# Time steps projected ahead of z, and their sums, columns and the scan's first transposes made beside the projection of z

## The chip, the cores and the metric

The kernel runs on one core of one Trainium2 chip. The metric is the device time of one execution in microseconds; the kernel before was run three times.

## The reference, cut to what matters

One step of an encoder layer on 512 new tokens of a prompt and 64 of a running stream: a mixer, attention over memory tokens, and a mixture of 16 experts. The change is in the mixer's state-space (Mamba-2) branch:

```python
h = rmsnorm(x, norm_mix)
z, xbc_raw, dt_raw, q, k, v, gl_ssm, gl_sb = split_cols(h @ w_in)
xbc = silu(causal_conv(xbc_raw))                    # 1536 channels: x, B, C
dt = softplus(dt_raw + dt_bias)                     # 16 heads: the time steps
a = -exp(a_log)
cum = cumsum(dt * a)                                # in blocks of positions
y, h_last = ssd_chunked(xh, dt, a, bm, cm, ssm_h0)  # the scan
y = y + d_skip[:, None] * xh
y_ssm = rmsnorm(y * silu(z), ssm_norm) @ w_ssm_br   # z: 1024 channels
```

So the scan needs dt and the convolved x, B, C; z is needed only where the scan's output is multiplied by it.

## The kernel before, in words

All 576 tokens (T = 512 + 64) are kept transposed, channels in the partitions, in 8 blocks of 128 channels (KD). The kernel writes its engines' programs out by hand: each engine runs its list in order, and semaphores are the only links between them.

**Weights.** `w_in` is cut into tiles of 8 x 128 x 256 words (or 128 columns), numbered in the order of use: K, V, Q, X (six tiles, 1536 columns of x, B, C), Z (four tiles, 1024 columns), DT (one tile, 128 columns, of which 16 are the time steps), then two tiles for each of the 8 merge steps (W_M on). SP loads tile n into one of four ring slots once tile n - 4 has been used for the last time (`load`, L1280; the table `retire`, L468). Each product is made in three passes of a high and a low part: `split_high` (L417, cast at L422) writes the high part on ScalarE, into one of two slots, once tile n - 2 has been used; `split_low` (L424, at L428) subtracts it in place on VectorE.

**Projections.** `tproj` (L1988, matmuls at L1985) makes 128 output channels of all tokens: 2 halves of 288 tokens x 8 blocks x 3 passes = 48 matmuls, the halves in two neighbouring PSUM banks. X takes 12 such steps, Z 8, DT one; they alternate between banks 0, 1 and banks 2, 3. For X, ScalarE copies out (L1483 to L1485), VectorE makes the convolution (L1728 to L1732), and ScalarE applies Silu (L1491). For Z, ScalarE applies Silu on the way out of PSUM (L1495) and signals `zt_ready`. After the last z step TensorE makes the columns of the D skip (L2160) and transposes the rows kept for the convolution (L2165), then the time steps' projection, and then transposes the initial state (L2175) once `dve_dt` 1 says that the time steps have been read.

**Row chain.** The time steps are 16 rows. VectorE adds the bias (L1750); ScalarE applies Abs, Exp and Ln (L1501 to L1505); VectorE adds the parts (L1757), multiplies by a (L1761), makes the sums by a scan instruction (L1763) and a diagonal of the last ones (L1766, `dve_dt` 7), and splits the sums in three bf16 parts (L1768 to L1776, `dve_dt` 12). TensorE turns sums and steps into columns (L2180, L2181) and spreads the last ones over all partitions (L2182); VectorE copies them out and copies the state (L1783), and ScalarE applies two exponentials (L1509, L1511).

**The scan** has 10 steps: 5 blocks of up to 128 tokens x 2 groups of 8 heads. In TensorE's order `ssd_first` of step v + 1 stands ahead of `ssd_second` of step v. `ssd_first` (L2197 to L2205) transposes x and B, makes the product of B and C, and spreads the sums. ScalarE makes decays from them (L1518, eight of L1520, L1524), GpSimd one product (L1386), VectorE the operands (`xdt`, L1797 to L1801) and the masked decays (L1811). `ssd_second` (L2219 to L2231) accumulates the output in bank 3 and the state in bank 6; VectorE multiplies the output into z (L1820) and updates the state (L1823, L1827). Banks: 7 and 0 for `ssd_first`, 1, 2 and 4, 5 in turn for the spread sums. VectorE does the low half of tile W_M + 1 in step 0. After the scan the final states are transposed (L2245) and the merge begins.

## Time and profile before

| | us |
|---|---|
| median of 3 runs | 1280.15 |
| lowest and highest run | 1276.65, 1280.24 |
| the profiled execution's own time | 1275.22 |
| its span | 1273.4 |
| TensorE busy (matmul) | 1159.3 (91%) |
| VectorE busy | 721.1 (57%) |
| ScalarE busy | 569.6 (45%) |
| GpSimd busy | 119.8 (9%) |
| mean granted clock of TensorE | 0.954 |

The profile is of one execution; its times count from the span's start. An engine's busy share says how long it had something running, not whether that was what the next work waited for. Overlapping matmuls are counted once, and their ends are modelled. In a timeline each row merges instructions of one line; the bracket gives the engine's idle time ahead of it and what ended that.

### The profile page before, as it was taken

What the parts mean: (1) busy time and instruction counts of PE and PEld (TensorE: products, weight loads), DVE (VectorE), ACT (ScalarE), POOL (GpSimd) and SP (SyncE); (2) the same over time, 40 slices, a digit from 0 to 9 for tenths busy, and PEclk for the clock granted to TensorE, in tenths of its full rate; (3) what the DMA queues carried; (4) which work ended last, traced back from release to release, by engine and by line L of the source; (5) the groups of instructions that cost most, each with busy time, mean ns of one, the idle gap of its engine ahead of it and who ended that gap; (6) DMA issues with size and microseconds to landing.
All of it is one profiled execution on the core that took longest, in us unless ns stands there. A gap on an engine that the chain in (4) does not pass through costs nothing.

```text
span 1273.4 us, 18213 instructions
## 1 busy us (share of the span) xinstructions
PE 1159.3 (91%) x7804; PEld 1041.8 (82%) x7813; DVE 721.1 (57%) x832; ACT 569.6 (45%) x704; POOL 119.8 (9%) x131
## 2 busy tenths in 40 slices
PE   5998997999969999999899899789769999899995
PEld 4997687999957899999899899469747777778873
DVE  5312764664168843342434713633478998888884
ACT  4423562332247642222315523421156687677763
POOL 1000431000034200000000000000010110000031
PEclk9998887999979999999999999999869999999998
DMA  8432000231310133332526612000389999999996
GB/s 277 137 105 66 1 1 17 67 96 55 83 35 2 34 91 83 81 93 68 174 68 221 210 38 84 12 17 34 130 317 339 422 399 385 360 395 392 366 286 155
DMA packets 95004, 197.24 MB, mean 155 GB/s; under 512 B 4184, under 2 KB 71928, under 8 KB 82632
## 3 DMA queue, kind: packets, MB, share of 16 engines
q1 hardware_dynamic: 87328, 169.88, 38.3%
q0 software_dynamic: 5408, 18.76, 5.0%
q10 hardware_dynamic: 2184, 7.39, 1.4%
q8 instruction: 63, 1.03, 0.3%
q14 instruction: 21, 0.17, 0.0%
HBM read 178.41 MB, written 17.60 MB: 154 GB/s over the span
## 4 chain that ended last, share of the span: by engine, by line
PE 69%; DVE 20%; ACT 7%; issue 3%; DMA 1%; POOL 0%; SPq 0%; ACTq 0%; DVEq 0%; POOLq 0%
PE ps L1985 44%; DVE buf_r L847 9%; PE ps L909 6%; PE ps L919 2%; ACT buf_r L840 2%; PE ps L2352 1%; PE ps L2103 1%; DVE buf_r L1028 1%; PE ps L2104 1%; DMA buf<-in_w_in 1%; PE ps L2074 1%; PE ps L539 1%; DVE buf L577 1%; PE ps L893 1%; ACT buf_r L422 1%
## 5 line engine op out<-in xcount | busy, mean ns | idle before, releaser
L1985 PE MATMUL ps<-buf_r,buf_r 128*128 128x288 f32 (+1 forms) x4560 | 595.5, 292 | 12.8 <-DVE buf_r L438 9.7
L1985 PEld LDWEIGHTS ps<-buf_r,buf_r 128*128 128x128 f32 x4560 | 589.1, 190 | 14.7 <-issue 5.9
L428 DVE TENSOR_TENSOR buf_r<-buf,buf_r 128x2048 fp32r<-128x2048 f32 (+2 forms) x53 | 116.6, 2200 | 174.8 <-ACT buf_r L422 174.8
L847 DVE TENSOR_TENSOR buf_r<-buf,buf_r 128x2048 fp32r<-128x2048 f32 x96 | 213.9, 2283 | 0.0
L909 PE MATMUL ps<-buf_r,buf_r 128*128 128x512 f32 x768 | 187.7, 400 | 6.9 <-DVE buf_r L1028 6.9
L840 ACT CAST buf_r<-buf 128x2048 fp32r<-128x2048 f32 x96 | 178.8, 1908 | 12.8 <-DMA buf<-in_w_gate_e 11.3
L909 PEld LDWEIGHTS ps<-buf_r,buf_r 128*128 128x128 f32 x768 | 144.0, 191 | 38.3 <-DVE buf_r L1028 7.7
L422 ACT CAST buf_r<-buf 128x2048 fp32r<-128x2048 f32 (+2 forms) x53 | 96.6, 1823 | 117.2 <-PE ps L1985 65.9
L919 PE MATMUL ps<-buf_r,buf_r 128*128 128x512 f32 x384 | 92.4, 395 | 2.5 <-DVE buf_r L1052 1.4
L919 PEld LDWEIGHTS ps<-buf_r,buf_r 128*128 128x128 f32 x384 | 71.8, 188 | 20.4 <-DVE buf_r L847 2.4
L434 ACT CAST buf_r<-ps 128x1024 fp32r<-128x1024 f32 (+1 forms) x32 | 25.7, 802 | 75.4 <-PE ps L893 66.7
L519 ACT ACTIVATE buf<-buf 128x1024 f32<-128x1024 f32 (+1 forms) x22 | 23.2, 1056 | 66.0 <-DVE buf L1966 48.1
L1074 POOL DMA_INDIRECT buf<-hn_rows,buf x16 | 23.3, 1453 | 270.2 <-DVE buf L583 135.2
L2103 PE MATMUL ps<-buf_r,buf_r 128*128 128x256 f32 (+1 forms) x78 | 30.0, 394 | 7.1 <-DVE buf_r L1678 7.1
L434 ACT CAST buf_r<-buf 128x576 fp32r<-128x576 f32 (+4 forms) x28 | 24.3, 869 | 23.6 <-DVE buf L1860 11.6
L438 DVE TENSOR_TENSOR buf_r<-buf,buf_r 128x576 fp32r<-128x576 f32 (+4 forms) x28 | 27.6, 999 | 10.2 <-ACT buf_r L434 10.2
L539 PE MATMUL ps<-buf,buf 128*128 128x128 f32 (+1 forms) x136 | 19.6, 296 | 12.2 <-DVE buf L529 9.5
L1386 POOL TENSOR_TENSOR buf<-buf,buf 128x1024 f32<-128x1024 f32 x10 | 27.9, 2785 | 29.5 <-ACT buf L1518 29.5
L1732 DVE SCALAR_TENSOR_TENSOR buf<-buf,buf,buf 128x579 f32<-128x579 f32 x36 | 29.6, 822 | 1.3
L1483 ACT COPY buf<-ps 128x288 f32<-128x288 f32 x12 | 4.8, 400 | 55.2 <-PE ps L1985 55.2
L2074 PE MATMUL ps<-buf,buf 64*128 64x512 f32 (+3 forms) x64 | 24.8, 540 | 4.6 <-DVE buf L1668 3.2
L1028 DVE TENSOR_TENSOR buf_r<-ps,buf_r 128x1024 fp32r<-128x1024 f32 x16 | 19.5, 1221 | 15.6 <-ACT buf_r L434 15.6
(313 smaller groups left out, 1208.6 us busy)
## 6 DMA issues: line engine op xcount, KB each, us to landing
buf<-in_w_gate_e SPq DMA_DIRECT2D x32, 1024.0 KB, 8.4
buf<-in_w_up_e SPq DMA_DIRECT2D x32, 1024.0 KB, 7.9
buf<-in_w_down_e SPq DMA_DIRECT2D x32, 1024.0 KB, 7.5
buf<-in_w_in SPq DMA_DIRECT2D x16, 1024.0 KB, 5.7
buf<-in_w_in SPq DMA_DIRECT2D x17, 512.0 KB, 4.7
buf<-in_w_mem_kv SPq DMA_DIRECT2D x8, 1024.0 KB, 5.7
y_rows<-buf ACTq DMA_DIRECT2D x14, 512.0 KB, 8.6
buf<-in_x_prompt SPq DMA_DIRECT2D x8, 512.0 KB, 5.3
```

Source lines behind the costliest of these rows:

```text
L422: nc.scalar.copy(w_hi(n), tile_view(RAW[n % NRAW], n)).then_inc(wh_ready, 1)
L428: nc.vector.tensor_tensor(r32(raw), raw, w_hi(n), ALU.subtract).then_inc(wl_ready, 1)
L434: nc.scalar.copy(r32(hi), src).then_inc(ah_ready, 1)
L539: last = nc.tensor.transpose(norm_banks(i, b0)[:, c, 0:n], src[:, c * P:(c + 1) * P], IDENT[:n, :n])
L840: nc.scalar.copy(e_hi(t), e_raw(t)).then_inc(wh_ready, 1)
L847: nc.vector.tensor_tensor(e_lo(t), e_raw(t), e_hi(t), ALU.subtract).then_inc(wl_ready, 1)
L909: last = nc.tensor.matmul(bank(b), r32(a[:, k, :]), w[:, i, :], start=(k == 0 and j == 0), stop=(k == KD - 1 and j == 2))
L919: last = nc.tensor.matmul(bank(5 + c), r32(a[:, k, :]), w[:, i, 512 * c:512 * (c + 1)], start=(k == 0 and j == 0), stop=(k == 3 and j == 2))
L1028: nc.vector.tensor_tensor(r32(GT[e % 2]), bank(0, 2).rearrange("p (c n) -> p c n", c=KD), r32(GTH[e % 2]), ALU.subtract).then_inc(al_ready, 1)
L1985: last = nc.tensor.matmul(out, a, b, start=(k == 0 and j == 0), stop=(k == len(parts) - 1 and j == 2))
L2074: last = nc.tensor.matmul(ps[:, o:o + n], KTA[r, hp, kc * P:(kc + 1) * P], QT[r, hp, kc * P:LP], start=True, stop=True)
L2103: nc.tensor.matmul(out, m, high[:, oj:oj + nj], start=(j == kc), stop=False)
```

## The change

The time steps' weight tile is numbered ahead of z's four, so it is loaded, split and projected between X and Z. z's eight steps use banks 3, 4 and 5, 6 in place of 0 to 3 (the last one 3 and 6), which leaves out banks 0, 1, 2 and 7; `tproj` takes a second bank. TensorE's order becomes: time steps, z0, D columns, tail transposes, state transposes, z1, z2, columns and spread, z3 to z6, `ssd_first(0)`, z7, then the scan as before, whose `ssd_second(0)` also waits for z7's Silu. ScalarE does the three row functions ahead of z0's Silu, the two exponentials behind z4's, z7's behind its part of scan step 0, and the cast of tile W_M + 1 behind its part of step 2. Silu is made in two instructions, one per bank. VectorE has the row chain ahead of and between the low halves of z's tiles, and the low half of W_M + 1 in step 4. The diff:

```diff
--- before.py
+++ after.py
@@ -385,8 +385,8 @@
         W_V = add_tiles(w_in, C_V, 512)
         W_Q = add_tiles(w_in, C_Q, 512)
         W_X = add_tiles(w_in, C_X, CONV_C * P)
+        W_DT = add_tiles(w_in, C_DT, P, P)
         W_Z = add_tiles(w_in, C_Z, D)
-        W_DT = add_tiles(w_in, C_DT, P, P)
         W_M = len(tiles)
         for c in range(0, D, P):
             tiles.append(([(0, cols(w_in, C_GS + c, P)), (8, cols(w_in, C_GB + c, P))], P))
@@ -1410,6 +1410,8 @@
             act_high(HTH[:, :, t0:t0 + n], HT[:, :, t0:t0 + n])
 
 
+        Z_BANK = [(3, 4), (5, 6)] * 3 + [(3, 4), (3, 6)]
+
         def cum_banks(v):
             return bank(1 if v % 2 == 0 else 4, 2).rearrange("p (h t) -> p h t", h=8)
 
@@ -1490,12 +1492,6 @@
                     act.wait_ge(conv_done, j + 1)
                     nc.scalar.activation(XC[:, j, 0:LP], CV[j % 2][:, 0:512], ACT.Silu)
                     nc.scalar.activation(XC[:, j, LP:T], CV[j % 2][:, 515:579], ACT.Silu).then_inc(xc_ready, 1)
-            for i in range(KD):
-                act.wait_ge(zt_psum, i + 1)
-                nc.scalar.activation(halves(ZS[:, i, :]), pair(2 * (i % 2)), ACT.Silu).then_inc(zt_ready, 1)
-                if i % 2:
-                    split_high(act, W_Z + 2 + i // 2)
-
             exp_and_ln()
             act.wait_ge(dve_dt, 1)
             nc.scalar.activation(AD[0:NH, :], UD[0:NH, :], ACT.Abs).then_inc(act_dt, 1)
@@ -1504,11 +1500,23 @@
             act.wait_ge(act_dt, 2)
             nc.scalar.activation(AD[0:NH, :], AD[0:NH, :], ACT.Ln, bias=1.0).then_inc(act_dt, 1)
             nc.scalar.activation(HCOL[0:NH, 3:4], HCOL[0:NH, 1:2], ACT.Exp).then_inc(act_dt, 1)
-            split_high(act, W_M + 1)
-            act.wait_ge(pre_dve, 4)
-            nc.scalar.activation(TE, TE, ACT.Exp).then_inc(pre_act, 1)
-            act.wait_ge(pre_psum, 2)
-            nc.scalar.activation(CD, bank(7)[:, 160:240].rearrange("p (c h) -> p c h", c=NC_), ACT.Exp).then_inc(pre_act, 1)
+            split_high(act, W_Z + 1)
+
+            def z_out(i):
+                act.wait_ge(zt_psum, i + 1)
+                for h in range(2):
+                    last = nc.scalar.activation(ZS[:, i, T // 2 * h:T // 2 * (h + 1)], bank(Z_BANK[i][h])[:, 0:T // 2], ACT.Silu)
+                last.then_inc(zt_ready, 1)
+
+            for i in range(KD - 1):
+                z_out(i)
+                if i in (1, 3, 5):
+                    split_high(act, W_Z + 2 + i // 2)
+                if i == 4:
+                    act.wait_ge(pre_dve, 4)
+                    nc.scalar.activation(TE, TE, ACT.Exp).then_inc(pre_act, 1)
+                    act.wait_ge(pre_psum, 2)
+                    nc.scalar.activation(CD, bank(7)[:, 160:240].rearrange("p (c h) -> p c h", c=NC_), ACT.Exp).then_inc(pre_act, 1)
             for v in range(10):
                 c, g = divmod(v, 2)
                 act.wait_ge(cumb_psum, v + 1)
@@ -1522,6 +1530,10 @@
                 last.then_inc(seg_done, 1)
                 act.wait_ge(seg_done, v + 1)
                 nc.scalar.activation(SEG[v % 2], SEG[v % 2], ACT.Exp, scale=-1.0).then_inc(e_ready, 1)
+                if v == 0:
+                    z_out(KD - 1)
+                if v == 2:
+                    split_high(act, W_M + 1)
             act.wait_ge(intra_psum, 10)
             act_high(YSBTH, YSBT)
             act.wait_ge(so_psum, 2)
@@ -1735,9 +1747,8 @@
                     o.then_inc(conv_step if j < 3 else conv_done, 1)
                 if i % 2:
                     split_low(dve, W_X + 2 + i // 2)
-            for n in range(W_Z + 2, W_M + 1):
-                split_low(dve, n)
-
+            dve.wait_ge(dt_psum, 1)
+            nc.vector.tensor_scalar(halves(UD[0:NH, :]), pair(0, NH), HCOL[0:NH, 0:1], None, ALU.add).then_inc(dve_dt, 1)
             dve.wait_ge(vec_ready, 3)
             for r in (0, 32, 64):
                 nc.vector.tensor_copy(SEL3[r:r + NH, :], IDENT[r:r + NH, r:r + NH])
@@ -1745,14 +1756,13 @@
             nc.vector.tensor_copy(DP, bank(7)[:, 240:248]).then_inc(vec_ready, 1)
             for s in range(2):
                 dve.wait_ge(dp_psum, 3)
-                nc.vector.tensor_copy(TAILR[0:36, s, :], bank(6)[0:36, P * s:P * (s + 1)]).then_inc(tail_rows, 1)
-            dve.wait_ge(dt_psum, 1)
-            nc.vector.tensor_scalar(halves(UD[0:NH, :]), pair(0, NH), HCOL[0:NH, 0:1], None, ALU.add).then_inc(dve_dt, 1)
+                nc.vector.tensor_copy(TAILR[0:36, s, :], bank(2)[0:36, P * s:P * (s + 1)]).then_inc(tail_rows, 1)
 
             nc.vector.memset(DTT[0:NH, T:TS], 0.0)
             nc.vector.memset(RST[0:NH, :], 1.0).then_inc(dve_dt, 1)
             dve.wait_ge(dve_dt, 2)
             nc.vector.memset(RST[0:NH, :].rearrange("p (c t) -> p c t", t=P)[:, :, 0:1], 0.0).then_inc(dve_dt, 1)
+            split_low(dve, W_Z + 1)
             dve.wait_ge(act_dt, 3)
             nc.vector.scalar_tensor_tensor(out=DTT[0:NH, 0:T], in0=UD[0:NH, :], scalar=0.0, in1=AD[0:NH, :],
                                            op0=ALU.max, op1=ALU.add).then_inc(dve_dt, 1)
@@ -1774,18 +1784,21 @@
             nc.vector.tensor_tensor(RST[64:64 + NH, :], DTA[32:32 + NH, :], CUM3[32:32 + NH, :], ALU.subtract).then_inc(dve_dt, 1)
             dve.wait_ge(dve_dt, 11)
             nc.vector.tensor_copy(CUM3[64:64 + NH, :], RST[64:64 + NH, :]).then_inc(dve_dt, 1)
+            split_low(dve, W_Z + 2)
             dve.wait_ge(pre_psum, 2)
             p7 = lambda a: bank(7)[:, a:a + 80].rearrange("p (c h) -> p c h", c=NC_)
             nc.vector.tensor_copy(CR, p7(0)).then_inc(pre_dve, 1)
             nc.vector.tensor_copy(DR, p7(80)).then_inc(pre_dve, 1)
             dve.wait_ge(pre_psum, 1)
             dve.wait_ge(pads, 2)
-            nc.vector.tensor_copy(HS[:, 1], bank(1, 2).rearrange("p (g n) -> p g n", g=2)).then_inc(pre_dve, 1)
+            nc.vector.tensor_copy(HS[:, 1], bank(0, 2).rearrange("p (g n) -> p g n", g=2)).then_inc(pre_dve, 1)
             dve.wait_ge(pre_dve, 3)
             nc.vector.tensor_tensor(TE, p7(160), CR, ALU.subtract).then_inc(pre_dve, 1)
+            split_low(dve, W_Z + 3)
             dve.wait_ge(pre_act, 2)
             nc.vector.tensor_tensor(WRW, DR, TE, ALU.mult).then_inc(pre_dve, 1)
             dve.wait_ge(pre_dve, 5)
+            split_low(dve, W_M)
 
             def xdt(v):
 
@@ -1812,10 +1825,12 @@
                                         ALU.mult).then_inc(m_ready, 1)
                 if v < 9:
                     xdt(v + 1)
-                if v == 0:
+                if v == 4:
                     split_low(dve, W_M + 1)
                 dve.wait_ge(intra_psum, v + 1)
                 n = CH[c][1]
+                if v == 1:
+                    dve.wait_ge(zt_ready, KD)
                 zv = ZS[:, 4 * g:4 * g + 4, c * P:c * P + n]
                 nc.vector.tensor_tensor(zv, zv, bank(3).rearrange("p (j t) -> p j t", j=4)[:, :, 0:n],
                                         ALU.mult).then_inc(yz_done, 1)
@@ -1985,11 +2000,11 @@
                     last = nc.tensor.matmul(out, a, b, start=(k == 0 and j == 0), stop=(k == len(parts) - 1 and j == 2))
             return last
 
-        def tproj(b, n, c, high, low, nk=KD, k0=0):
+        def tproj(b, n, c, high, low, nk=KD, k0=0, b2=None):
 
             for h in range(2):
                 t = slice(h * (T // 2), (h + 1) * (T // 2))
-                last = passes(bank(b + h)[:, 0:T // 2], [((w_hi(n)[:, k0 + k, c:c + P], w_lo(n)[:, k0 + k, c:c + P]),
+                last = passes(bank(b2 if h and b2 else b + h)[:, 0:T // 2], [((w_hi(n)[:, k0 + k, c:c + P], w_lo(n)[:, k0 + k, c:c + P]),
                                      (r32(high[:, k, t]), r32(low[:, k, t]))) for k in range(nk)])
             return last
 
@@ -2145,15 +2160,22 @@
                 if i >= 2:
                     pe.wait_ge(xr_ready, i - 1)
                 tproj(2 * (i % 2), W_X + i // 2, (i % 2) * P, HTH, HT).then_inc(xb_psum, 1)
-            for i in range(KD):
+            pe.wait_ge(wl_ready, W_DT + 1)
+            pe.wait_ge(xr_ready, CONV_C - 1)
+            tproj(0, W_DT, 0, HTH, HT).then_inc(dt_psum, 1)
+
+            def z_rows(i):
                 if i % 2 == 0:
                     pe.wait_ge(wl_ready, W_Z + i // 2 + 1)
-                if i < 2:
-                    pe.wait_ge(xr_ready, CONV_C - 1 + i)
-                else:
-                    pe.wait_ge(zt_ready, i - 1)
-                tproj(2 * (i % 2), W_Z + i // 2, (i % 2) * P, HTH, HT).then_inc(zt_psum, 1)
-
+                if i == 0:
+                    pe.wait_ge(xr_ready, CONV_C)
+                if i == 1:
+                    pe.wait_ge(ysb_ready, 5)
+                if i >= 2:
+                    pe.wait_ge(zt_ready, i - 1 if i < KD - 1 else i)
+                tproj(Z_BANK[i][0], W_Z + i // 2, (i % 2) * P, HTH, HT, b2=Z_BANK[i][1]).then_inc(zt_psum, 1)
+
+            z_rows(0)
             pe.wait_ge(vec_ready, 4)
             pe.wait_ge(ysb_ready, 5)
             for j in range(8):
@@ -2162,18 +2184,15 @@
             last.then_inc(dp_psum, 1)
             pe.wait_ge(conv_done, CONV_C)
             for s in range(2):
-                nc.tensor.transpose(bank(6)[0:36, P * s:P * (s + 1)], TAIL[:, s].rearrange("p j c -> p (j c)"),
+                nc.tensor.transpose(bank(2)[0:36, P * s:P * (s + 1)], TAIL[:, s].rearrange("p j c -> p (j c)"),
                                     IDENT).then_inc(dp_psum, 1)
-            pe.wait_ge(wl_ready, W_DT + 1)
-            pe.wait_ge(zt_ready, 7)
-            tproj(0, W_DT, 0, HTH, HT).then_inc(dt_psum, 1)
-
             pe.wait_ge(state_loaded, 16)
             pe.wait_ge(dve_dt, 1)
-            pe.wait_ge(zt_ready, 8)
             for b in range(8):
-                last = nc.tensor.transpose(bank(1, 2)[:, b * P:(b + 1) * P], H0R[:, b, :], IDENT)
+                last = nc.tensor.transpose(bank(0, 2)[:, b * P:(b + 1) * P], H0R[:, b, :], IDENT)
             last.then_inc(pre_psum, 1)
+            z_rows(1)
+            z_rows(2)
             pe.wait_ge(dve_dt, 7)
             pe.wait_ge(vec_ready, 5)
             for c in range(NC_):
@@ -2181,6 +2200,8 @@
                 nc.tensor.transpose(bank(7)[:, 80 + 16 * c:96 + 16 * c], DTT[0:NH, c * P:(c + 1) * P], IDENT[0:NH, 0:NH])
             nc.tensor.matmul(bank(7)[:, 160:240], ONES[0:NH, :], DIAG[0:NH].rearrange("p c h -> p (c h)"),
                              start=True, stop=True).then_inc(pre_psum, 1)
+            for i in range(3, KD - 1):
+                z_rows(i)
             pe.wait_ge(pre_dve, 4)
             pe.wait_ge(pre_act, 2)
             pe.wait_ge(xc_ready, CONV_C)
@@ -2216,6 +2237,7 @@
                 else:
                     pe.wait_ge(dd_ready, 2)
                     pe.wait_ge(pads, 3)
+                    pe.wait_ge(zt_ready, KD)
                 nc.tensor.matmul(bank(3), ZERO[:, 0:P], ZERO, start=True, stop=False)
                 for j in range(4):
                     nc.tensor.matmul(bank(3)[:, j * P:(j + 1) * P], DD[g][:, j, :], XC[:, 4 * g + j, tk], start=False, stop=False)
@@ -2233,6 +2255,7 @@
                 last.then_inc(intra_psum, 1)
 
             ssd_first(0)
+            z_rows(KD - 1)
             for v in range(10):
                 if v + 1 < 10:
                     ssd_first(v + 1)
```

## Rows read from the trace of the kernel before

**Rows 1.** The page, part 4: the chain that ended last, shares of the span.

```profile
PE 69%; DVE 20%; ACT 7%; issue 3%; DMA 1%; POOL 0%; SPq 0%; ACTq 0%; DVEq 0%; POOLq 0%
```

**Rows 2.** Timeline of TensorE before the scan: start, duration, operation, idle time before it.

```profile
346.04 1.94 PE L2160 MATMUL ps<-buf,buf 16*128 16x1 f32 x16
...
348.06 6.60 PE L1985 MATMUL ps<-buf_r,buf_r 128*128 128x288 f32 x48
355.61 1.06 PE L2175 MATMUL ps<-buf,buf 128*128 128x128 f32 x8 [0.94 <-issue]
360.91 0.28 PE L2180 MATMUL ps<-buf,buf 16*128 16x16 f32 x1 [4.24 <-DVE buf L1766]
...
367.20 1.09 PE L2197 MATMUL ps<-buf,buf 128*128 128x128 f32 x4 [4.51 <-ACT buf L1511]
...
370.77 1.11 PE L2197 MATMUL ps<-buf,buf 128*128 128x128 f32 x4 [0.99 <-DVE buf L1801]
```

**Rows 3.** Timeline of TensorE in the scan.

```profile
379.97 1.05 PE L2221 MATMUL ps<-buf,buf 128*128 128x128 f32 x8 [0.33 <-DVE buf L1820]
...
384.27 1.09 PE L2231 MATMUL ps<-buf,buf 128*64 128x128 f32 x16 [1.16 <-DVE buf L1811]
385.86 0.66 PE L2197 MATMUL ps<-buf,buf 128*128 128x128 f32 x4 [0.50 <-DVE buf L1801]
...
387.36 1.05 PE L2221 MATMUL ps<-buf,buf 128*128 128x128 f32 x8
...
391.44 0.66 PE L2197 MATMUL ps<-buf,buf 128*128 128x128 f32 x4
...
428.81 1.09 PE L2231 MATMUL ps<-buf,buf 128*64 128x128 f32 x16
```

**Rows 4.** Stretches: length, busy times (instructions) of each engine, granted clock, DMA.

```profile
348.00:354.70 6.70, 6.66 (x50) 6.42 (x50) 3.25 (x7) 1.87 (x2) 1.07 (x2) 1.00 0.57 152
...
360.90:367.20 6.30, 1.78 (x13) 1.60 (x13) 4.88 (x10) 0.40 (x2) 3.09 (x4) 0.50 0.00 0
...
378.00:386.00 8.00, 6.00 (x64) 4.49 (x62) 7.90 (x10) 4.21 (x11) 2.36 (x1) 1.00 0.00 0
```

**Rows 5.** Timeline of ScalarE around the projection of z.

```profile
295.16 0.40 ACT L1483 COPY buf<-ps 128x288 f32<-128x288 f32 x1 [4.94 <-PE ps L1985]
...
301.53 0.65 ACT L1495 ACTIVATE buf<-ps 128x576 f32<-128x576 f32 x1 [1.47 <-PE ps L1985]
...
346.69 1.89 ACT L422 CAST buf_r<-buf 128x2048 fp32r<-128x2048 f32 x1
...
369.81 1.02 ACT L1518 ACTIVATE buf<-ps 128x1024 f32<-128x1024 f32 x1 [2.72 <-PE ps L2205]
...
372.94 1.06 ACT L1524 ACTIVATE buf<-buf 128x1024 f32<-128x1024 f32 x1
```

**Rows 6.** Timeline of VectorE, same stretch and the scan's start.

```profile
299.17 2.29 DVE L428 TENSOR_TENSOR buf_r<-buf,buf_r 128x2048 fp32r<-128x2048 f32 x1
...
354.70 0.81 DVE L1750 TENSOR_SCALAR buf<-ps,buf 16x576 f32<-16x576 f32 x1 [2.80 <-PE ps L1985]
...
360.62 0.23 DVE L1766 TENSOR_TENSOR buf<-buf,buf 16x80 f32<-16x80 f32 x1
...
376.76 2.33 DVE L428 TENSOR_TENSOR buf_r<-buf,buf_r 128x1536 fp32r<-128x1536 f32 x1
...
381.00 3.21 DVE L1811 TENSOR_TENSOR buf<-buf,buf 128x1024 f32<-128x1024 f32 x1
...
387.71 1.22 DVE L1811 TENSOR_TENSOR buf<-buf,buf 128x1024 f32<-128x1024 f32 x1
```

**Rows 7.** Timeline of GpSimd at the scan's second step.

```profile
380.78 2.36 POOL L1386 TENSOR_TENSOR buf<-buf,buf 128x1024 f32<-128x1024 f32 x1 [3.30 <-ACT buf L1518]
```

**Rows 8.** Timeline of ScalarE behind the scan.

```profile
446.02 1.28 ACT L1545 ACT_TABLE_LOAD   x1
447.31 0.65 ACT L1545 ACTIVATE buf<-ps 128x576 f32<-128x576 f32 x1
```

## The prediction

> **What bounds the kernel now.** I read the page's chain first: TensorE carries 69% of what ended last [rows 1], so time is to be had where TensorE stands still and something else is last. TensorE's timeline ahead of the scan shows three such places: 0.94 us before the state's transposes, 4.24 us before the columns, 4.51 us before the scan, and 0.99 us more before the scan's second step [rows 2]. In sum 10.68 us. The releasers named are VectorE's row chain (L1766), the exponentials on ScalarE (L1511) and VectorE's operands (L1801): the reader is to see a serial chain over 16 rows that starts only when the time steps are out of PSUM. The scan's timeline comes next, for the pace of its undisturbed steps and for three smaller stops of 0.33, 1.16 and 0.50 us [rows 3]. Last the granted clock by stretches: 1.00 until 354.7, 0.50 in 360.9 to 367.2 with TensorE busy 1.78 of 6.3 us, 1.00 again from 378 [rows 4]. So the stops also make TensorE slow behind them: the same four transposes take 1.09 us at 367.2 and 0.66 us at 385.9 [rows 2, 3].
>
> **The stretch that I sum.** It begins where the last x/B/C projection is done, which the copy at 295.16 shows [rows 5], and ends with the scan's last matmuls at 428.81 + 1.09 = 429.90 [rows 3]: 134.7 us. Before it nothing is changed but the order of two tile loads. Behind it the same waits follow the scan's end.
>
> **TensorE's work after the change, in its new order.** One projection of 128 columns takes 301.53 - 295.16 = 6.37 us [rows 5]. Nine of them (time steps and z0 to z7) are 57.3 us. The D-skip columns and tail transposes are 348.06 - 346.04 = 2.0 us, the state's transposes 1.1 [rows 2], the columns 1.8 (busy time in that stretch) [rows 4]. In the scan a "first" takes 387.36 - 385.86 = 1.50 us and a "second" 391.44 - 387.36 = 4.08 us at full clock [rows 3]. First(0) to first(3) and second(0) and (1) are 4 x 1.50 + 2 x 4.08 = 14.2 us; from second(2) at 387.36 to 429.90 I take the 42.5 us as they are, with what waits they hold. Sum 118.9 us. The durations of the small groups are taken whole, though behind another matmul their tails overlap; that may give 0.5 us more.
>
> **Does a wait take the place of the old ones?** I lay the new order on the clock of the old trace.
> - Time steps 295.2 to 301.5. z0 needs the low half of z's first tile. Tile 13 is still the one split at 299.17 + 2.29 = 301.46 [rows 6], and is now needed at once, not one tile later: TensorE's start hangs on it with 0.05 us to spare. I put 0.1 us there, between 0 and 0.5.
> - z0 ends at 307.9, small groups and state at 311.1. The state's transposes wait for the time steps to leave banks 0 and 1: 0.81 us on VectorE [rows 6], so by 302.4, long before.
> - z1 to 317.5. z2 needs tile 14. ScalarE does the three 16-row functions first (576 columns each, as Silu's 0.65 us [rows 5], so some 2.1 us, to 304.5), then the cast, 1.89 us. VectorE stands at the D columns until TensorE has passed z0 (309.9). Of its 3.25 busy us in 348.0 to 354.7 the copies there were 1.0 beside a low half of 2.29 [rows 4, 6]; the memsets I put at 1 more. Ready at 309.9 + 2.0 + 2.3 = 314.2, 3.3 us early.
> - z2 to 323.9. The columns need dve_dt 7. The row chain was 354.70 to 360.62 + 0.23 = 360.85, 6.15 us in all [rows 6]; without the first row (0.81) and ScalarE's 2.1 it has 3.2 left behind the low half, so 317.4: 6.5 us early. The 4.24 us stop goes. The three-part sums behind it are asked for at 351 only.
> - z3 from 325.7, z4 at 332.0. Its tile waits for z1 to retire (317.5), then Silu, cast and low half, 0.7 + 1.9 + 2.3: 322.4, 9.6 us early. z6 at 344.8 has its tile from z3's end at 332.0 + 4.9 = 336.9, 7.9 us early. The wait of z by its banks is for the step two before, and the copy-out is 0.65 us [rows 5].
> - The exponentials of TE and CD come behind z4's Silu, at about 341, ten us before the scan. The 4.51 us stop goes. z6 ends at 351.1.
> - First(0) to 352.6, then z7 to 359.0. Beside z7 ScalarE does its whole first scan step, 374.00 - 369.81 = 4.2 us [rows 5], and VectorE its operands: the 0.99 us goes. z7's Silu must be out before second(0), which TensorE reaches at 360.5: it ends about 0.75 us after z7, at 359.8. ScalarE's second step then ends by about 365.2 with VectorE 1.2 us behind it; second(1) asks for it 3.1 us after 366, at 369.
>
> **Table loads.** Silu and Exp now alternate, by my reading of the new order six more switches than before, each 1.28 us, with the next function 0.01 us after it [rows 8]. They stand ahead of the semaphore wait in ScalarE's idle time, or behind a step that has 6.37 us of cover. In the scan two of them count, one on either side of z7's Silu; with 1.28 us each they meet the times above (ScalarE free at 357.5, table at 358.8). Uncovered, the two would be 2.6 us. I take 0.
>
> The Trainium skill ("ScalarE: Activation LUTs", What ACT_TABLE_LOAD costs) gives each switch about 1.28 us and a drain of about 1.38 us more, which speaks against this change. Rows 8 show the first and not the second. By the page, z7's Silu would end 0.4 us after second(0) is reached, and the sum below would be 0.4 us smaller. I go by the rows.
>
> **The stops inside the scan.** Before, VectorE did the low half of the second branch tile (L428, 2.33 us, GpSimd's share in it included) in step 0. With it VectorE came late, met GpSimd's product at 380.78 (2.36 us) and took 3.21 us for one at 381.00 that takes 1.22 at 387.71 [rows 6, 7]; TensorE stopped 0.33 + 1.16 + 0.50 = 1.99 us [rows 3]. The change moves this low half to step 4. It stands at the same place of its step there, behind the next step's operands, so I expect the same meeting and the same 1.99 us there: moved, not saved. Bounds 0 and 4 us. On ScalarE the cast of that tile moves behind step 2 (1.5 us, against 5.58 - 4.2 = 1.4 us free per step): nothing waits for that.
>
> **SP's queue.** Each load waits for the tile four before it. With the time steps' tile in front, the loads of the later tiles are released by z1, z3, z5 and z7 at the latest; none is needed within 10 us. Cost 0.
>
> **Sum.** 118.9 + 0.1 + 2.0 = 121.0 us against 134.7 us: 13.7 us less. Of it 10.7 are the idle times of rows 2, and 3.0 are the low clock, which has no stop left to follow. The profiled execution took 1275.22 us (span 1273.4), so it would take 1261.5. The median of the three runs is 4.9 us above that execution; 1280.15 - 13.7 = 1266.4, and I predict 1266 us.
>
> **Rivals.**
> - *Half of it comes back in the scan.* The first steps run late on ScalarE and VectorE because z7, its Silu, two tables and the delayed steps crowd there, and the low half in step 4 costs the upper bound. 2.6 + 2 + 2 us are 6.6 us back: 1273 us. For it: VectorE's waits in the scan are short, and 0.2 us of bad phase cost 2.0 us there [rows 6, 7]. Against: 6.4 us of z7 lie over step 0. Chance 0.16.
> - *The change does not do what it says*: the chain still ends after TensorE is through, because VectorE, in one queue, is held by the D columns, pads or a tile. It would have to be 6.5 us later than I find at the columns and over 9 us at the exponentials. Then about 10 us remain of the stops: 1278 us. Chance 0.06.
> - *Slower: the clock falls in the middle of z.* The mechanism: the 16-row matmuls, transposes and waits now stand between z0 and z1 and between z2 and z3, and the clock falls there as it fell at 355 to 361. At the low level a projection takes 6.37 x (1.09 / 0.66) = 10.5 us, 4.1 us more. From four such steps on it is slower than before; with five, 1266 + 21 = 1287 us. Against it: through 348.0 to 354.7, right behind the same small matmuls, the clock stayed at 1.00 [rows 4]. Chance 0.03.
>
> **How the numbers follow.** The forecast has 0.75. Its own range is the sum's bounds: 0.5 us of overlap and 2.0 us of step 4 gained, 2 to 3 us lost there and at z0, and the 3 us by which runs of this kernel differ: 1260.5 to 1271. Reached out to the first rival the range is 1260.5 to 1274. Runs of this kernel tell differences from about 0.3%, 3.8 us: faster holds the forecast, the first rival and a little of the second (0.91), same most of the second (0.06), slower the third (0.03).
>
> **What would show it.** In the new profile: no idle time of TensorE over 0.3 us between 295 and the scan; the time steps' projection at 295.2 with its row function at 301.5; clock 1.00 in every stretch from 295 to 430; z7's projection between first(0) and first(1); the last scan matmuls ending at about 416; a VectorE product of some 3 us and stops of about 2 us at step 4; everything behind the scan moved up by the same 13.7 us. The prediction is wrong if TensorE stands at z2, z4 or z6, if ScalarE's first steps in the scan are what second(0) or second(1) waits for, or if the stages behind the scan give time back.

## The result and the profile after

The changed kernel's median was 1263.39 us (4 runs, 1255.01 to 1266.45) against 1278.40 us (4 runs): ratio 0.9899, interval 0.986 to 0.9937. A second set of 6 runs beside 11 of the kernel before gave 0.9906 (0.9872 to 0.9941). The profiled execution took 1261.06 us, its span 1259.3. Forecast were 1266 us, and 13.7 us less in the stretch from the end of the x/B/C projection to the end of the scan.

The whole is noisy, its parts are not. First the kernel before, then the changed one, by stages between the same events: the tail of the attention (unchanged), the stretch, the merge's start, and a part of the expert stage. Columns as in [rows 4].

```profile
191.00:223.00 32.00, 24.86 (x210) 22.84 (x209) 14.20 (x18) 7.52 (x6) 4.72 (x4) 0.80 0.06 17
...
295.16:429.90 134.74, 120.91 (x1042) 107.53 (x1050) 73.40 (x113) 62.09 (x128) 32.34 (x16) 0.94 0.15 40
429.90:457.40 27.50, 25.47 (x191) 24.53 (x189) 20.31 (x26) 21.86 (x26) 1.88 (x2) 1.00 0.29 77
...
959.67:1100.00 140.33, 134.19 (x659) 107.07 (x658) 127.82 (x122) 99.38 (x71) 13.28 (x10) 1.00 0.99 387
```

```profile
191.00:219.20 28.20, 21.06 (x210) 18.96 (x210) 14.45 (x18) 7.52 (x6) 4.73 (x4) 0.96 0.06 19
...
291.34:411.60 120.26, 117.18 (x1042) 104.21 (x1051) 73.61 (x113) 71.26 (x142) 32.98 (x16) 1.00 0.18 49
411.60:439.10 27.50, 25.47 (x190) 24.53 (x189) 20.32 (x26) 21.85 (x26) 1.88 (x2) 1.00 0.29 77
...
942.52:1085.00 142.48, 135.90 (x660) 108.35 (x659) 129.66 (x123) 99.40 (x72) 13.30 (x10) 0.99 0.98 382
```

The stretch went from 134.74 to 120.26 us, 14.5 less, with TensorE busy 117.2 of 120.3 us and the clock at 1.00, not 0.94. The attention's tail was 3.8 us shorter, with the clock at 0.96 and not 0.80, before any changed instruction; the merge's start was equal; the later stages were 4.2 us longer, of which 2.2 in the piece shown. These two nearly cancel in this pair of profiles, which is luck. The last experiment shows that the first is chance, and leaves open whether some 2 us of the second are.

TensorE in the changed kernel. `tproj`'s matmuls are at L2000 now, the D columns at L2182, the state's transposes at L2192, the sums' columns at L2199 to L2201, `ssd_first` at L2218 to L2226, `ssd_second` at L2243 to L2253.

```profile
304.25 1.94 PE L2182 MATMUL ps<-buf,buf 16*128 16x1 f32 x16
...
306.36 1.04 PE L2192 MATMUL ps<-buf,buf 128*128 128x128 f32 x8
307.15 12.96 PE L2000 MATMUL ps<-buf_r,buf_r 128*128 128x288 f32 x96
320.04 0.23 PE L2199 MATMUL ps<-buf,buf 16*128 16x16 f32 x1
...
320.69 0.42 PE L2201 MATMUL ps<-buf,buf 16*128 16x80 f32 x2
321.04 25.76 PE L2000 MATMUL ps<-buf_r,buf_r 128*128 128x288 f32 x192
346.63 0.60 PE L2218 MATMUL ps<-buf,buf 128*128 128x128 f32 x4
...
347.82 6.62 PE L2000 MATMUL ps<-buf_r,buf_r 128*128 128x288 f32 x48
354.29 0.60 PE L2218 MATMUL ps<-buf,buf 128*128 128x128 f32 x4
...
355.72 1.05 PE L2243 MATMUL ps<-buf,buf 128*128 128x128 f32 x8
...
384.61 1.05 PE L2243 MATMUL ps<-buf,buf 128*128 128x128 f32 x8 [1.04 <-DVE buf L1835]
...
388.29 1.09 PE L2253 MATMUL ps<-buf,buf 128*64 128x128 f32 x16 [0.55 <-DVE buf L1824]
389.88 0.66 PE L2218 MATMUL ps<-buf,buf 128*128 128x128 f32 x4 [0.50 <-DVE buf L1814]
...
410.51 1.09 PE L2253 MATMUL ps<-buf,buf 128*64 128x128 f32 x16
```

The rows up to 384 have no bracket, so TensorE has no idle time to speak of between 304 and 384, where [rows 2] had 0.94, 4.24, 4.51 and 0.99 us. Two projections lie between the state's transposes and the columns, four (25.76 us) up to the scan, z7 (6.62 us) between the first two `ssd_first`, and the four transposes take 0.60 us, not 1.09. The three stops of [rows 3], 0.33 and 1.16 us in `ssd_second(1)` and 0.50 us ahead of `ssd_first(3)`, are now 1.04 and 0.55 us in `ssd_second(5)` and 0.50 us ahead of `ssd_first(7)`, one step behind the low half, which VectorE now does in its step 4. The scan ends at 410.51 + 1.09 = 411.60.

ScalarE beside it: row functions, cast, and Silu with its table changes.

```profile
298.56 0.69 ACT L1497 ACTIVATE buf<-buf 16x576 f32<-16x576 f32 x1 [1.01 <-DVE buf L1751]
...
300.68 1.89 ACT L422 CAST buf_r<-buf 128x2048 fp32r<-128x2048 f32 x1
302.59 1.28 ACT L1508 ACT_TABLE_LOAD   x1
304.36 0.71 ACT L1508 ACTIVATE buf<-ps 128x288 f32<-128x288 f32 x2 [0.48 <-PE ps L2000]
...
334.81 1.28 ACT L1517 ACT_TABLE_LOAD   x1
336.11 0.27 ACT L1517 ACTIVATE buf<-buf 128x80 f32<-128x80 f32 x1
...
353.06 1.28 ACT L1508 ACT_TABLE_LOAD   x1
354.49 0.71 ACT L1508 ACTIVATE buf<-ps 128x288 f32<-128x288 f32 x2
355.21 1.28 ACT L1526 ACT_TABLE_LOAD   x1
356.51 1.02 ACT L1526 ACTIVATE buf<-ps 128x1024 f32<-128x1024 f32 x1
```

The table load at 302.59 stands ahead of its wait for z0. The two in the scan (353.06, 355.21) lie around z7's Silu, which is out at 355.20, half a microsecond ahead of the first "second" at 355.72.

### The profile page after: what moved, and what is told of

It is laid out like the page before. It is cut to its first block, busy times and chain, and to the rows that moved or that the text cites. A ratio compares the mean times of both kernels' runs of the same rounds, so it can differ in the third digit from the quotient of the medians.

```text
span 1259.3 us, 18228 instructions
## 1 busy us (share of the span) xinstructions
PE 1157.4 (92%) x7804; PEld 1038.5 (82%) x7813; DVE 720.4 (57%) x832; ACT 578.0 (46%) x718; POOL 120.2 (10%) x131
## 4 chain that ended last, share of the span: by engine, by line
PE 69%; DVE 19%; ACT 6%; issue 3%; DMA 1%; POOL 0%; SPq 0%; ACTq 0%; DVEq 0%; POOLq 0%
PE ps L2000 45%; DVE buf_r L847 9%; PE ps L909 6%; PE ps L919 2%; ACT buf_r L840 2%; PE ps L2375 1%; PE ps L2118 1%; DVE buf_r L1028 1%; DMA buf<-in_w_in 1%; PE ps L2089 1%; PE ps L2119 1%; PE ps L539 1%; DVE buf L577 1%; PE ps L893 1%; ACT buf_r L422 1%
## 5 line engine op out<-in xcount | busy, mean ns | idle before, releaser
L2000 PE MATMUL ps<-buf_r,buf_r 128*128 128x288 f32 (+1 forms) x4560 | 598.1, 293 | 12.8 <-DVE buf_r L438 9.7
L2000 PEld LDWEIGHTS ps<-buf_r,buf_r 128*128 128x128 f32 x4560 | 591.1, 191 | 15.0 <-issue 5.9
L909 PE MATMUL ps<-buf_r,buf_r 128*128 128x512 f32 x768 | 189.0, 402 | 7.1 <-DVE buf_r L1028 7.1
L422 ACT CAST buf_r<-buf 128x2048 fp32r<-128x2048 f32 (+2 forms) x53 | 96.7, 1824 | 117.2 <-PE ps L2000 65.9
L919 PE MATMUL ps<-buf_r,buf_r 128*128 128x512 f32 x384 | 94.0, 400 | 2.6 <-DVE buf_r L1052 1.4
L1462 ACT ACTIVATE buf<-buf 128x1280 f32<-128x1280 f32 x10 | 12.7, 1270 | 35.1 <-POOL buf L1352 18.7
```

What stands on the lines that cost most here:

```text
L422: nc.scalar.copy(w_hi(n), tile_view(RAW[n % NRAW], n)).then_inc(wh_ready, 1)
L909: last = nc.tensor.matmul(bank(b), r32(a[:, k, :]), w[:, i, :], start=(k == 0 and j == 0), stop=(k == KD - 1 and j == 2))
L919: last = nc.tensor.matmul(bank(5 + c), r32(a[:, k, :]), w[:, i, 512 * c:512 * (c + 1)], start=(k == 0 and j == 0), stop=(k == 3 and j == 2))
L2000: last = nc.tensor.matmul(out, a, b, start=(k == 0 and j == 0), stop=(k == len(parts) - 1 and j == 2))
```

## The experiments

Each was read by its stretch, from the last 288-column copy of the x/B/C projection to the scan's last matmul. This has next to no scatter: three profiles of the kernel before gave 134.74 or 134.75 us each, two of the changed kernel 120.25 and 120.28.

**Stops without the low clock.** Dummy matmuls in both long stops of the kernel before:

```diff
             last.then_inc(pre_psum, 1)
+            for _ in range(28):
+                nc.tensor.matmul(bank(5)[:, 0:T // 2], r32(HTH[:, 0, 0:P]), r32(HTH[:, 0, 0:T // 2]), start=True, stop=True)
             pe.wait_ge(dve_dt, 7)
 ...
                              start=True, stop=True).then_inc(pre_psum, 1)
+            for _ in range(30):
+                nc.tensor.matmul(bank(5)[:, 0:T // 2], r32(HTH[:, 0, 0:P]), r32(HTH[:, 0, 0:T // 2]), start=True, stop=True)
             pe.wait_ge(pre_dve, 4)
```

> The kernel before, with 28 matmuls of 128x288 (133 ns each) into an unused bank behind the state's transposes and 30 behind the columns; nothing reads them. They fill TensorE's two long stops (4.24 and 4.51 us) without shortening what is waited for. Theory: of the 14.5 us that the changed kernel saved between the x/B/C projection and the scan's end, about 3 are the low clock behind the stops. Then here the clock stays at 1.00 over the whole stretch, the chain of VectorE and ScalarE takes the same time, and the stretch (134.7 us) falls by 2.5 to 3.5 us, to about 131.7. Rival: the clock behind the stops costs nothing by itself, because the first scan steps wait for VectorE and ScalarE anyway: stretch 134.7, scan's second step at the same distance from the row chain.

Stretch 133.68 us: 1.1 less, not 3. Time 0.9975 of the kernel before (0.995 to 0.9999). Its TensorE, VectorE and GpSimd:

```profile
362.20:368.40 6.20, 5.21 (x42) 4.90 (x42) 4.80 (x9) 0.40 (x2) 2.99 (x4) 1.00 0.00 0
...
371.30:376.00 4.70, 4.64 (x43) 3.61 (x46) 1.86 (x4) 4.67 (x14) 3.06 (x2) 1.00 0.00 0
...
368.49 0.63 PE L2201 MATMUL ps<-buf,buf 128*128 128x128 f32 x4 [1.07 <-DVE buf L1785]
...
371.30 0.66 PE L2201 MATMUL ps<-buf,buf 128*128 128x128 f32 x4 [1.40 <-DVE buf L1801]
...
380.11 1.05 PE L2225 MATMUL ps<-buf,buf 128*128 128x128 f32 x8 [1.66 <-DVE buf L1820]
...
383.44 1.10 PE L2232 MATMUL ps<-buf,buf 128*128 128x512 f32 x2 [1.25 <-DVE buf L1827]
...
379.75 2.75 DVE L1823 TENSOR_TENSOR buf<-buf,buf 128x512 f32<-128x512 f32 x1
...
379.59 2.36 POOL L1386 TENSOR_TENSOR buf<-buf,buf 128x1024 f32<-128x1024 f32 x1 [1.98 <-ACT buf L1518]
```

The clock is 1.00 throughout, the scan starts where it did (72.05 us into the stretch, 72.04 before), and the second `ssd_first` comes 0.75 us sooner. The third, at 377.02, comes 2.46 us sooner (80.58 us into the stretch, 83.04 before): so much work time did the low clock cost, close to the 2.5 to 3.5 of the theory. But then TensorE waits 1.66 us for VectorE, which has the low half of tile W_M + 1 from 376.88 to 379.23, and 1.25 us more because VectorE's `hs` product (L1823, the state's update) at 379.75 finds GpSimd's, which began 0.16 us before it, and takes 2.75 us, not 0.68. TensorE stops 1.66 + 1.25 + 0.50 = 3.4 us in place of 2.0. So 1.4 of the 2.5 us came back as stops: a full clock alone is worth 1.1 us in this order, neither the 3 of the theory nor the 0 of the rival.

**Columns and exponentials behind z.** The columns' block, both exponentials and the copies moved behind z7, z7 ahead of the scan (TensorE's part is shown; ScalarE's and VectorE's are moved to match):

```diff
             z_rows(1)
             z_rows(2)
+            for i in range(3, KD):
+                z_rows(i)
             pe.wait_ge(dve_dt, 7)
             pe.wait_ge(vec_ready, 5)
 ...
-            for i in range(3, KD - 1):
-                z_rows(i)
 ...
             ssd_first(0)
-            z_rows(KD - 1)
```

> The changed kernel with the columns, the two exponentials and the state's copy behind z7 and not between z2 and z3; row chain, state transposes and D columns stay beside z; z7 is ahead of the scan. Theory (each serial piece costs what TensorE then stands still): from z7's end 1.0 us of columns, then VectorE's copies and ScalarE's exponentials, 2.5 to 3 us of idle TensorE before the scan, 0.8 to 1 us before its second step, and 0 to 1 us of low clock: the stretch (120.3 us) grows by 3.5 to 5 us. Rival (it was mainly the row chain that had to be ahead; the columns cost little): under 1.5 us.

Stretch 127.48 us, 7.2 more; ratio 0.9952 (0.9929 to 0.9976). 0.80 us of it is my edit's own: z7 kept its banks 3 and 6 and so waited for z6's Silu. The rest is 6.4 us, above the 3.5 to 5 expected:

```profile
352.75 0.63 PE L2215 MATMUL ps<-buf,buf 128*128 128x128 f32 x4 [2.36 <-DVE buf L1795]
...
355.56 1.12 PE L2215 MATMUL ps<-buf,buf 128*128 128x128 f32 x4 [0.99 <-DVE buf L1811]
...
358.39 1.91 PE L2240 MATMUL ps<-buf,buf 128*128 128x128 f32 x8 [0.22 <-issue]
...
355.50:360.00 4.50, 4.22 (x23) 4.29 (x24) 1.19 (x3) 4.47 (x13) 2.58 (x2) 0.50 0.02 4
```

Idle are 2.36, 0.99 and 0.22 us, 3.6 together. Of the other 2.8 us, 2.5 are the low clock by the times of the same matmuls in the changed kernel, where 0 to 1 was expected: it is 0.50 from 355.5 to 360 (eight matmuls take 1.91 us, not 1.05). It was down already behind the stop of 2.36 us and ahead of the second stop: the eight matmuls of L2223 at 353.55 take 1.02 us, not 0.61. Putting only the row chain ahead would not have done: 6.4 of the 14.5 us hang on what follows it, z7 in the scan among them.

**z7 ahead of the scan.** First with its own banks, then with banks 5 and 6 (there `ssd_first(1)`, which needs bank 5, also waits for z7's Silu; that was out 1.8 us before it started):

```diff
-            for i in range(3, KD - 1):
+            for i in range(3, KD):
                 z_rows(i)
 ...
             ssd_first(0)
-            z_rows(KD - 1)
```

> The changed kernel with z7 and its Silu ahead of the scan's first step and not between its first two. Theory: z7 covers VectorE's operands (1.8 us) and ScalarE's first step with a table load (5.3 us): without it TensorE stands about 1 us before the second step and 0 to 1 us for the masked decays or the table load: stretch 120.3 plus 1 to 2.5 us. Rival (z7 in the scan crowds ScalarE with two table loads and gains nothing): stretch unchanged or up to 0.5 us shorter.

> The earlier version with z7 ahead of the scan, its banks now 5 and 6 so that it need not wait for z6's Silu (that wait was 0.80 us of the 3.55 us which the earlier version lost against the changed kernel). Theory: the rest, 2.7 us, is what z7 covers in the scan: 1.33 us for VectorE's operands, 0.55 for GpSimd's product, 0.34 for the operands again, and what is left around them. Stretch 120.3 + 2.7 = 123.0. Rival: the wait for z6 had only delayed things that wait elsewhere: stretch 123.8.

Stretches 123.81 and 122.77 us: z7 in the scan is worth 2.5 us, near the expected 2.7. The second version's stops:

```profile
360.84 0.66 PE L2218 MATMUL ps<-buf,buf 128*128 128x128 f32 x4 [1.33 <-DVE buf L1812]
...
363.93 1.09 PE L2246 MATMUL ps<-buf,buf 128*64 128x128 f32 x16 [0.54 <-POOL buf L1386]
...
367.43 0.66 PE L2218 MATMUL ps<-buf,buf 128*128 128x128 f32 x4 [0.33 <-DVE buf L1812]
```

1.33 + 0.54 + 0.33 = 2.2 us: VectorE's operands, GpSimd's product, and the operands again. Ratios 0.994 (0.9915 to 0.9965) and 0.9897 (0.9844 to 0.9949).

**No table loads.** z without its Silu, copied:

```diff
-                    ... bank(Z_BANK[i][h])[:, 0:T // 2], ACT.Silu)
+                    ... bank(Z_BANK[i][h])[:, 0:T // 2], ACT.Copy)
```

> The changed kernel with a plain copy in place of Silu on z (z is left without its Silu). The copy takes the same time and needs no table of its own, so the six extra table loads around z vanish. Theory: each load is 1.28 us with nothing behind it and all lie in ScalarE's free time: stretch 120.3, within 0.2 us. Rival (a switch also costs a drain, or the two loads in the scan hold step 1): stretch shorter by 0.5 us or more.

Stretch 120.25 us against 120.26: the six loads cost nothing. (Ratio 0.9932, 0.99 to 0.9965.)

**The low half in quarters.**

```diff
-                if v == 4:
-                    split_low(dve, W_M + 1)
+                if 3 <= v <= 6:
+                    split_low_part(dve, W_M + 1, v - 3, 4)
```

`split_low_part`, not shown here, subtracts one quarter and signals with the last.

> The changed kernel with the low half of the second branch tile done in four quarters in scan steps 3 to 6 and not whole in step 4. Theory: the stops of 1.04, 0.55 and 0.50 us around step 4 come from VectorE being 1.5 us late once and then meeting GpSimd's product; a quarter of some 0.5 us fits into VectorE's 0.8 us of free time per step. Then all three go: stretch 120.3 less 2.1 us, 118.2, no VectorE product over 1.3 us. Rival: four fixed costs and the place behind the operands make VectorE late in each of four steps: GpSimd is met more often, stretch 120.3 or longer.

Stretch 120.17 us: the rival came true. Ratio 0.989 (0.9843 to 0.9938). VectorE and GpSimd in it:

```profile
375.78 1.13 DVE L436 TENSOR_TENSOR buf_r<-buf,buf_r 128x384 fp32r<-128x384 f32 x1
...
389.76 0.69 DVE L1852 TENSOR_TENSOR buf<-buf,ps 128x512 f32<-128x512 f32 x1
390.36 3.33 DVE L1834 TENSOR_TENSOR buf<-buf,buf 128x1024 f32<-128x1024 f32 x1
...
395.22 0.54 DVE L436 TENSOR_TENSOR buf_r<-buf,buf_r 128x384 fp32r<-128x384 f32 x1
...
390.25 2.36 POOL L1396 TENSOR_TENSOR buf<-buf,buf 128x1024 f32<-128x1024 f32 x1 [2.21 <-ACT buf L1536]
```

A quarter takes 0.54 us with GpSimd idle (395.22) and 1.13 us while GpSimd has its product (375.78): it waits for that to end. Each makes VectorE some 0.2 us later, and when GpSimd's product starts 0.11 us before the masked decays (390.25, 390.36) these take 3.33 us, not 1.22, and TensorE stops 0.22, 1.28 and 0.50 us.

**The low half early.** The cast goes behind z7's Silu and the low half into step 0, where VectorE waits 3 us:

```diff
                 if v == 0:
                     z_out(KD - 1)
-                if v == 2:
                     split_high(act, W_M + 1)
 ...
-                if v == 4:
+                if v == 0:
                     split_low(dve, W_M + 1)
```

> The changed kernel with the cast of the second branch tile right behind z7's Silu and its low half in scan step 0, where VectorE stands for 3.0 us (from 356.9) while TensorE is in its first 'second'. Theory: what stopped TensorE at step 4, and in the quartered version at steps 5 and 6, was VectorE being more than 0.4 us late for the masked decays, so that GpSimd's product went first. Here the low half (1.6 us) ends before VectorE is asked for: no stop of 0.3 us or more from the second step on except the 0.5 us at the last; stretch 120.3 less 2 us, 118.2 (up to 118.8 if ScalarE's cast makes step 1 late). Rival: the meeting only moves again, because the cast puts ScalarE and with it GpSimd 1.5 us late in step 1: stretch 120 to 122.

Stretch 118.18 us, 2.1 less than the changed kernel, with no stop of TensorE from z0 on but the 0.5 us ahead of the last step. Ratio 0.9837 (0.9797 to 0.9877), whose interval overlaps the changed kernel's.

**One table load at the merge.** The same, with the set of Ln and Exp loaded ahead of the token scale:

```diff
             def token_scale():
+                exp_and_ln()
                 act.wait_ge(ssq_psum, 1)
```

> As the early-low version, and with the table set that holds both Ln and Exp loaded once ahead of the token scale, in place of one load before each function. In the changed kernel's chain these are 1.28 + 1.28 us behind the first branch projections, and TensorE then stands 1.13 us. Theory: one load goes and the other may lie ahead of the wait: TensorE's stop at the merge's second step goes, 1.1 us less behind the scan (27.5 us there become 26.4), beside the 2 us of the other version. Rival: the stop stays, since the cast and the low half behind it were last: 27.5 us.

Stretch 118.15 us, and at the merge TensorE no longer stops:

```profile
434.36 11.88 PE L2000 MATMUL ps<-buf_r,buf_r 128*128 128x288 f32 x87
...
435.01 1.28 ACT L1420 ACT_TABLE_LOAD   x1
436.30 0.74 ACT L1549 ACTIVATE buf<-ps,buf 128x576 f32<-128x576 f32 x1
437.08 0.69 ACT L1551 ACTIVATE buf<-buf 128x576 f32<-128x576 f32 x1
```

The same place in the changed kernel:

```profile
439.09 3.19 PE L2000 MATMUL ps<-buf_r,buf_r 128*128 128x288 f32 x22 [1.13 <-DVE buf_r L428]
```

There 1.13 us of idle time stood ahead of 439.09, with a load for Ln at 432.01 and one for Exp at 434.07 in ScalarE's queue before it; here one load at 435.01, Exp right behind Ln, and 87 matmuls without a gap. Ratio 0.9895 (0.9843 to 0.9947).

**Is anything given back behind the scan?** The two unchanged kernels again, and the last version again:

> The kernel before, unchanged, for a second profile. In the profiles so far the part behind the scan (from the scan's last matmul to the span's end) lasts 843.5 and 844.6 us in the two with the old order and 846.5 to 849.9 us in the seven with the new one. Theory: this is chance of TensorE's granted clock in the later stages, in which neither kernel differs; then this profile may lie anywhere in 843 to 850. Rival: the new order gives some 3 us back behind the scan; then this one is again at 843 to 845. The part ahead of the stretch (up to the end of the x/B/C projection, 286.9 to 296.5 us so far) is expected anywhere in that range, the stretch at 134.7 +- 0.2 us.

> The same once more: the part behind the scan anywhere in 843 to 850 us by the theory of chance, 843 to 845 by the rival; the stretch at 134.7 +- 0.2 us by both.

> The changed kernel, unchanged, for a second profile and more timed runs beside the kernel before. Stretch 120.3 +- 0.2 us; the part behind the scan anywhere in 843 to 850 us by the theory of chance, 846 or more by the rival. Time against the kernel before: 14.5 us less by the first (ratio 0.9887), about 11.5 us less by the second (0.9910).

> The version with the early low half and one table load at the merge, once more with more timed runs: stretch 118.2 us, 1.1 us less than the changed kernel behind it up to the merge's second step, so 17.7 us less than the kernel before if nothing is given back (ratio 0.9861), and 3.2 us less than the changed kernel.

| profile | ahead of the stretch | stretch | behind it | span |
|---|---|---|---|---|
| before | 295.2 | 134.7 | 843.5 | 1273.4 |
| before, again | 287.3 | 134.7 | 847.0 | 1269.0 |
| before, third | 290.7 | 134.7 | 846.8 | 1272.2 |
| changed | 291.3 | 120.2 | 847.7 | 1259.3 |
| changed, again | 290.2 | 120.3 | 844.7 | 1255.1 |
| early low half | 294.6 | 118.2 | 846.5 | 1259.3 |
| with one table load | 296.5 | 118.2 | 849.3 | 1263.9 |
| the same, again | 294.5 | 118.2 | 848.8 | 1261.4 |

The rival as it was put falls: with the old order the part behind the scan also took 847.0 us, with the new one also 844.7. The part ahead lies between 286.9 and 296.5 us over all profiles, in kernels of either order: that is chance. That nothing is given back behind the scan is not shown. Four profiles of the old order (the filled one too) have 843.5 to 847.0 us there, mean 845.4; ten of the new order have 844.7 to 849.9, mean 847.7. Split once more, at VectorE's first three products of L577 in a row (959.59 in the first profile), the part from the scan to there is equal, 529.4 and 529.6 us in the mean. The rest, in which the DMA engines are busy 0.88 to 0.99 of the time in the four profiles looked at, takes 313.8 to 317.2 us in the old order and 316.4 to 319.7 in the new. So some 2 of the 14.5 us may come back in the expert stage; with this scatter it can't be told from chance, and no cause was tried.

The whole runs lean the same way. The last version's ratio was 0.9896 (0.9862 to 0.9931), where 0.9861 was expected if nothing is given back; the changed kernel's beside it was 0.9906, where 0.9887 was expected. The last version is shorter by 3.2 us in the stages that were changed, but it can't be told apart in whole runs.

## Why the prediction was right

- *Where TensorE stood.* All four stops of [rows 2] went, 10.7 us, as forecast, and no wait took their place. Nothing was late that was said to be early: tile 14's low half ended at 310.2, TensorE came at 307.15 + 6.37 = 313.5 (3.3 us early, as forecast); the diagonal was there 6.7 us before the columns (forecast 6.5); z4's tile 8.6 us and z6's 7.6 us early (forecast 9.6 and 7.9).
- *z0's weights.* Forecast were 0.05 us to spare, with 0.1 put down. TensorE's matmuls stood 0.01 us, but the weight load ahead of them waited 0.25 us for this low half, and time steps and z0 together took 0.16 us more than two projections. So it was a little late, near the 0.1.
- *Small groups.* The state's transposes cost 0.8 us, not 1.1, and the columns 1.0, not 1.8. The 1.8 was the busy time of a stretch at clock 0.50 [rows 4], used for work that would run at full clock: the largest of the sum's errors, and about as large as the whole difference between 121.0 and 120.3. First(0) and first(1) took 1.19 and 1.43, not 1.50. The nine projections took 0.5 us more than nine times 6.37, which hides the rest.
- *The low clock.* 3.0 us were put down to it as what idle time did not explain. As part of a difference between these two kernels that stands, since the new order has no stop behind which it could fall. As a cost of its own it does so only in part: with the stops filled TensorE was 2.5 us ahead at the third `ssd_first`, and 1.1 us at the end, as in the old order part of a faster start only met the next waits.
- *The stop inside the scan.* Forecast: moved to step 4 with 1.99 us. Measured: 2.09 us right behind it. That the low half makes it is shown by its absence with the early low half. The sum came out right, its parts did not, so the 0.1 us is luck: 1.04 us (0.33 before) are a wait for the product with z (L1835), which stood behind the low half itself, and only the rest follows from VectorE's meeting with GpSimd, which had begun 0.92 us before and not 0.22 [rows 6, 7]:

```profile
381.40 2.33 DVE L428 TENSOR_TENSOR buf_r<-buf,buf_r 128x1536 fp32r<-128x1536 f32 x1
...
385.63 2.60 DVE L1824 TENSOR_TENSOR buf<-buf,buf 128x1024 f32<-128x1024 f32 x1
...
384.71 2.44 POOL L1386 TENSOR_TENSOR buf<-buf,buf 128x1024 f32<-128x1024 f32 x1 [2.60 <-ACT buf L1526]
```

- *Table loads.* Six more, as counted; cost 0 as taken. The Trainium skill's drain ("ScalarE: Activation LUTs", What ACT_TABLE_LOAD costs) would have added 0.4 us to the time, an estimate from that page's 1.38 us (where the prediction has the sum "smaller", it is the saving that would be). In the trace the load at 353.06 takes 1.28 us and Exp's first instruction at 356.51 starts 0.02 us behind the load before it; no drain is seen, and without the six loads the stretch was the same, 120.25 us.
- *The whole.* The median fell by 15.0 us in the first four runs and the ratio puts it at 0.6 to 1.4%: the 14.5 us of the stretch are 1.1%. The two ratios, 0.9899 and 0.9906, stand for 12.9 and 12.0 us, so that the 15.0 us between medians are partly chance. No rival came true. Of the signs of being wrong one stays open: the stages behind the scan may give 2 us back. The second rival's 1278 us was mis-added: 1266.4 and 10 us make 1276.4.

## What to carry to other kernels

A serial chain over a few rows is cheap when it starts a stage earlier: find what it really needs (one small projection), put that first, and give the next big block banks that the chain's outputs don't use. Before adding an instruction to an engine's loop that seems to have slack, look at what another engine does at that moment: a few tenths of delay can change which of VectorE and GpSimd goes first and cost 2 us; here one piece of work in a hole of 3 us was better than four quarters in holes of 0.8 us. When runs scatter more than the change, compare stages between events that both kernels have.

## What was not expected of the hardware

- VectorE products of two operands in SBUF and GpSimd's product exclude each other in whole instructions: 1.22 us became 3.33 us when GpSimd had begun 0.11 us before, and 2.60 us in step 5 of the changed kernel, when it had begun 0.92 us before. The Trainium skill ("SBUF — State Buffer", Terms) says that the loser of this port pair "**fully blocks**"; the trace agrees, and GpSimd's 2.36 us became 2.98 when it lost. A VectorE product with one operand in PSUM was not held up: L1842 at 385.03 took its usual 0.69 us while GpSimd's product ran from 384.71 to 387.15.
- Unchanged code ahead of the stretch took 286.9 to 296.5 us in the profiles. Between the first two the difference was the attention's tail, 32.0 us at clock 0.80 and 28.2 at 0.96; TensorE stood idle 7.14 us in both (32.00 - 24.86 and 28.20 - 21.06), so all 3.8 us are busy time at the lower clock. What sets the clock there was not tried.
